# The output stage of a decoder step: injections computed ahead of the tile loop, half of the routed rows paired on GpSimd, a ring of hidden tiles

## The reference, cut to what matters

```python
idx = top_k(...)                                  # 8 of 64 experts for each row
h = h + routed(rmsnorm(h, g_ffn)) + shared        # routed: weighted sum of 8 expert rows
h = h + (p @ w_ple_proj) * sigmoid(rmsnorm(h, g_ple) @ w_ple_gate)
y = rmsnorm(h, g_final)
```

## Time and profile before

| | us |
|---|---|
| median of 3 runs (1900.89 to 1901.89) | 1901.25 |
| profiled execution, its own time | 1903.72 |
| span of the profiled execution, first to last instruction | 1901.9 |
| PE busy, whole span | 1716.1 (90%) |
| DVE busy, whole span | 968.8 (51%) |
| ACT busy, whole span | 779.8 (41%) |
| POOL busy, whole span | 513.7 (27%) |
| mean granted clock of TensorE, of 1 | 0.962 |

### The profile page before, as it was taken

One profiled execution on the slowest core, in us unless ns is written; L12 is line 12 of the kernel. 1 busy time (PEld: TensorE's weight loads), 2 busy tenths in 40 slices (PEclk: granted clock), 3 DMA queues, 4 the chain that ended last, 5 costly groups with the idle time before them and its releaser, 6 DMA issues. The chain is left out here.

```text
span 1901.9 us, 25091 instructions
## 1 busy us (share of the span) xinstructions
PE 1716.1 (90%) x7154; PEld 1075.3 (57%) x7155; DVE 968.8 (51%) x1639; ACT 779.8 (41%) x1453; POOL 513.7 (27%) x733
## 2 busy tenths in 40 slices
PE   6999999978985699999999998999999999937998
PEld 4666666545774456556656655656665565623443
DVE  3333333314996354555444545445555544637885
ACT  2222222212331355665555555545556554721221
POOL 0000110000665332333332334223333322411221
PEclk9999999987998799999999998999999999978999
DMA  9200000021111787888777768767787776958650
GB/s 360 100 0 0 0 0 0 15 96 47 67 67 62 255 294 257 274 286 292 255 243 248 257 232 299 246 228 271 260 280 274 260 253 222 337 219 331 270 166 28
DMA packets 124013, 363.70 MB, mean 191 GB/s; under 512 B 28966, under 2 KB 44262, under 8 KB 121389
## 3 DMA queue, kind: packets, MB, share of 16 engines
q1 hardware_dynamic: 87909, 290.85, 44.2%
q0 software_dynamic: 35760, 72.49, 10.7%
q10 hardware_dynamic: 320, 0.07, 0.0%
HBM read 334.52 MB, written 71.91 MB: 214 GB/s over the span
## 5 line engine op out<-in xcount | busy, mean ns | idle before, releaser
L1409 PE MATMUL Y<-raw_d,hT 128*128 128x512 f32 (+1 forms) x768 | 352.1, 602 | 19.7 <-ACT hT L1469 19.7
L197 DVE TENSOR_TENSOR lo_gu<-raw_g,hi_gu 128x1024 fp32r<-128x1024 f32 x130 | 153.5, 1221 | 366.5 <-ACT hi_gu L190 321.3
L1367 PE MATMUL GU<-hi_gu,x_hi 128*128 128x512 f32 (+1 forms) x768 | 322.0, 419 | 5.7 <-issue 4.1
L1367 PE MATMUL GU<-hi_gu,x_lo 128*128 128x512 f32 (+1 forms) x768 | 304.6, 397 | 0.0
L1367 PE MATMUL GU<-lo_gu,x_hi 128*128 128x512 f32 (+1 forms) x768 | 304.3, 396 | 0.0
L1477 ACT ACTIVATE y<-Y,w_t 128x512 f32<-128x512 f32 (+1 forms) x256 | 168.3, 683 | 238.5 <-PE Y L1409 230.6
L1328 POOL DMA_INDIRECT y_dram<-y,to_row x128 | 131.3, 1026 | 472.0 <-ACT y L1477 354.0
L1409 PEld LDWEIGHTS Y<-raw_d,hT 128*128 128x128 f32 (+1 forms) x768 | 132.3, 179 | 178.7 <-issue 167.3
L1317 POOL DMA_INDIRECT rows<-rows_dram,from_row x131 | 159.0, 1214 | 109.1 <-POOL from_row L1315 76.8
L1367 PEld LDWEIGHTS GU<-hi_gu,x_hi 128*128 128x128 f32 (+1 forms) x768 | 136.8, 178 | 77.4 <-issue 39.6
L107 POOL TENSOR_SCALAR st<-st 128x1 f32<-128x1 f32 (+3 forms) x45 | 14.4, 321 | 582.5 <-ACT junk L585 201.0
(11 more groups left out here) (221 smaller groups left out, 2139.3 us busy)
## 6 DMA issues: line engine op xcount, KB each, us to landing
raw_g<-in_w_exp_gate SPq DMA_DIRECT2D x130, 512.0 KB, 5.9
raw_u<-in_w_exp_up SPq DMA_DIRECT2D x130, 512.0 KB, 6.2
raw_d<-in_w_exp_down SPq DMA_DIRECT2D x130, 512.0 KB, 4.9
yk<-y_dram SPq DMA_DIRECT2D x16, 2048.0 KB, 12.7
rows_dram<-row SPq DMA_DIRECT2D x9, 512.0 KB, 2.7
h_dram<-resid SPq DMA_DIRECT2D x9, 512.0 KB, 2.7
w_big<-in_w_in SPq DMA_DIRECT2D x2, 2048.0 KB, 12.8
w_out<-in_w_out SPq DMA_DIRECT2D x1, 4096.0 KB, 18.1
```

Of the source, the lines that this page charges most:

```text
L197: dve.tensor_tensor(part_of(keep, "lo", m, par, h), part_of(keep, "raw", m, par, h), part_of(keep, "hi", m, par, h).bitcast(F32), ALU.subt ...
L1367: ins = pe.matmul(out, lhs[x], rhs[w], start=first and i == 0, stop=last and i == 2)
L1409: ins = pe.matmul(Y[half][0:n, :], hT[b][:, f, :], raw_d[par][:, f, cols], start=f == 0, stop=f == FC - 1)
```

## The change

- The two norm weights `g_ple` and `g_fin` get buffers that live from the expert stage on, and SyncE loads them at its head, ahead of `ple`; it waits for them at that stage's end.
- Injections: ahead of the tile loop TensorE transposes the p rows of all nine tiles straight from `ple` (no copy on GpSimd) and multiplies them; ScalarE copies each half product from PSUM into `inject`, which holds all tiles in SBUF. VectorE's multiply and add are then one whole tile wide each.
- Routed rows: GpSimd adds row 5 to row 4 and row 7 to row 6 of a tile, in place in `yk`; VectorE adds rows 0 to 3 and the two pairs: six adds.
- Hidden tiles: a ring of four buffers `res` in place of `resid4`, loaded tile by tile. `out`, `colT` and `pT` get two buffers each, sums of squares and roots a column per tile.
- ScalarE copies both halves of the transposed row. TensorE puts the transposes of t+1 between the two halves of the gate product of t. All loops are written out.

The diff, cut to its core (declarations, and what only renames, left out):

```diff
@@ build @@
-            keep["ple"] = ctx.enter_context(nc.sbuf_tensor("ple", [P, TILES, PLE], F32, side="right"))
+            for name, shape in (("ple", [P, TILES, PLE]), ("g_ple", [P, D]), ("g_fin", [P, D])):
+                keep[name] = ctx.enter_context(nc.sbuf_tensor(name, shape, F32, side="right"))
@@ experts, SyncE @@
-            for dst, src in ((ple[:, 0:PROMPT_TILES, :], a["p_prompt"][0, 0].rearrange("(t p) d -> p t d", p=P)),
+            for dst, src in ((keep["g_ple"][:], a["g_ple"][0:1, :].broadcast_to([P, D])),
+                             (keep["g_fin"][:], a["g_final"].rearrange("(a d) -> a d", a=1).broadcast_to([P, D])),
+                             (ple[:, 0:PROMPT_TILES, :], a["p_prompt"][0, 0].rearrange("(t p) d -> p t d", p=P)),
...
+            sp.wait_ge(keep["output_ld"], 16 * 4)
@@ output, SyncE @@
+            def hidden(t):
+                sp.dma_start(res[t % RING][:], tiles[t]).then_inc(h_ld[t % RING], 16)
...
+            hidden(0)
+            routed(0)
+            hidden(1)
+            routed(1)
+            hidden(2)
+            hidden(3)
+            for t in range(TILES):
+                if t + 2 < TILES:
+                    sp.wait_ge(summed, t + 1)
+                    routed(t + 2)
+                if t >= 2:
+                    store(t - 2)
+                    if t + 2 < TILES:
+                        hidden(t + 2)
@@ output, GpSimd @@
+            def pair_up(t):
+                pool_after(pool, keep["passed"], y_ld[t % 2][1], 16 * (t // 2 + 1))
+                for k in (TOP // 2, TOP // 2 + 2):
+                    pool.tensor_tensor(yk[t % 2][:, k, :], yk[t % 2][:, k, :], yk[t % 2][:, k + 1, :], ALU.add).then_inc(
+                        paired, 1)
...
+            pair_up(0)
+            norm_in(0)
+            pair_up(1)
+            norm_in(1)
+            for t in range(TILES):
+                if t + 2 < TILES:
+                    pair_up(t + 2)
+                if t:
+                    norm_out(t - 1)
+                if t + 2 < TILES:
+                    norm_in(t + 2)
@@ output, TensorE @@
+            ple_transposes(0)
+            for t in range(TILES):
+                if t + 1 < TILES:
+                    ple_transposes(t + 1)
+                project(t)
+            transposes(0)
+            for t in range(TILES):
+                gates(t, 0)
+                if t + 1 < TILES:
+                    transposes(t + 1)
+                gates(t, 1)
@@ output, ScalarE @@
+            p_copy(0)
+            for t in range(TILES):
+                if t + 1 < TILES:
+                    p_copy(t + 1)
+                j_copy(t)
+                if t == 4:
+                    square_sum(0)
+            col_copy(0)
+            square_sum(1)
+            for t in range(TILES):
+                if t:
+                    final_sum(t - 1)
+                if t + 1 < TILES:
+                    col_copy(t + 1)
+                sigmoid(t, 0)
+                if t + 2 < TILES:
+                    square_sum(t + 2)
+                sigmoid(t, 1)
@@ output, VectorE @@
+            def total(t):
...
+                for k in range(TOP // 2):
+                    own.did(dve.tensor_tensor(r[:], r[:], y[:, k, :], ALU.add))
+                    own.wait()
+                for i in range(2):
+                    dve.wait_ge(paired, 2 * t + i + 1)
+                    ins = dve.tensor_tensor(r[:], r[:], y[:, TOP // 2 + 2 * i, :], ALU.add)
...
+            total(0)
+            norm(0)
+            total(1)
             for t in range(TILES):
+                if t:
+                    add_injection(t - 1)
+                if t + 1 < TILES:
+                    norm(t + 1)
                 if t + 2 < TILES:
+                    total(t + 2)
+                if t:
+                    finish(t - 1)
```

More of the change, by code:

```diff
@@ L1602, in chosen_rows @@
                     sp.dma_start(yk[t % 2][0:n, k, :], chosen[t, 0:n, k, :]).then_inc(y_ld[t % 2][q], 16)
[L1604 to L1608, removed]
@@ L1674, in transposes, with gates @@
                     ins.then_inc(x_tr, 1)
[L1676 to L1684, removed]
-                    transposes(t + 1)
[L1686 to L1702, removed]
+            def gates(t, h):
+                after(pe, g_ready, 2 * t + h - 1)
+                for k in range(KC):
+                    if h == 0 and k % 4 == 0:
+                        pe.wait_ge(x_ev, 2 * t + k // 4 + 1)
+                    ins = pe.matmul(G[h][:], colT[t % 2][:, k, :], w_gate[:, k, h * 512:(h + 1) * 512],
+                                    start=(k == 0), stop=(k == KC - 1))
+                ins.then_inc(g_done, 1)
+            pe.wait_ge(zeroed, 2)
+            ple_transposes(0)
[7 more added lines that the diff above has]
+                if t + 1 < TILES:
+                    transposes(t + 1)
+                gates(t, 1)
         @block.scalar
@@ L1732, in _, with j_copy @@
[L1732 to L1738, removed]
+                after(act, j_done, 2 * t - 2)
+                act.activation(pT[t % 2][:].rearrange("p f q -> p (f q)"), XP[:, 0:PLE], ACT.Copy).then_inc(p_ev, 1)
+            def j_copy(t):
+                for h in range(2):
+                    act.wait_ge(j_done, 2 * t + h + 1)
+                    act.activation(inject[:, t, h * 512:(h + 1) * 512], J[h][:], ACT.Copy).then_inc(j_ev, 1)
@@ new lines, in col_copy, with sigmoid @@
+            def col_copy(t):
+                for b in range(2):
+                    act.wait_ge(x_tr, 2 * t + b + 1)
+                    if b == 0:
+                        after(act, g_done, 2 * t - 2)
+                    act.activation(colT[t % 2][:, 4 * b:4 * b + 4, :], X[b][:].rearrange("p (k q) -> p k q", k=4),
+                                   ACT.Copy).then_inc(x_ev, 1)
+            def sigmoid(t, h):
+                act.wait_ge(g_done, 2 * t + h + 1)
+                if h == 0:
+                    after(act, injected, t)
+                act.activation(gate[:, h * 512:(h + 1) * 512], G[h][:], ACT.Sigmoid).then_inc(g_ready, 1)
@@ L1767, in inject, with add_injection @@
[L1767 to L1776 removed]
+            def add_injection(t):
+                dve.wait_ge(g_ready, 2 * t + 2)
+                dve.wait_ge(j_ev, 2 * t + 2)
+                own.did(dve.tensor_tensor(inj[:], gate[:], inject[:, t, :], ALU.mult))
+                own.wait()
+                dve.tensor_tensor(res[t % RING][:], res[t % RING][:], inj[:], ALU.add).then_inc(injected, 1)
@@ L1778, in finish @@
             def finish(t):
                 dve.wait_ge(fin_ready, t + 1)
-                dve.wait_ge(out_st, 16 * t + 16)
-                dve.scalar_tensor_tensor(out=out[:], in0=resid[:, t, :], scalar=st[:, 5:6], in1=g_fin[:],
+                after(dve, out_st[t % 2], 16 * (t // 2))
+                dve.scalar_tensor_tensor(out=out[t % 2][:], in0=res[t % RING][:], scalar=rs[:, 1, t:t + 1], in1=g_fin[:],
                                          op0=ALU.mult, op1=ALU.mult).then_inc(out_ready, 1)
-            def following(t, first, between):
-                gather_sum(t, range(first, TOP), t % 2)
-                between()
-                norm(t)
-                col_copy(t)
```

165 lines of the change are left out of this document (61 added, 104 removed).

## The result

The changed kernel takes 1890.3 us (median of 11 runs, 1887.8 to 1897.2) against 1900.9 (median of 11, 1898.6 to 1903.9): a ratio of 0.995, 95% interval 0.994 to 0.996. It is faster, by 10.6 us; 1892.5 was forecast, within 1876 to 1906.

The account below looks back on a forecast made before the run. VectorE and GpSimd as a pair were to bound the changed tile loop: first gate product 1728.8, tiles through 1881.5, tail to 1891.6, clock 1.5, span 1893.1; plus 1.8 less 2.5 gave 1892.5 us, range 1876 to 1906.

Parts of the forecast that it names:

- The opening: Ahead of the tile loop: injection products made in idle time, first gate product at 1728.8, 6 us later, at full clock.
- The price of GpSimd's add: GpSimd's new two-input add of 128x1024 tiles in the output stage: 2.2 us taken, between 1.0 and 2.65.
- the sum: VectorE's steady tile, sum to sum: its operations, two stalls of 1.95 and 0.2 of small norms, 18.05 us.
- The path to SBUF: Output stage: one engine holds SBUF's path a whole instruction; each GpSimd add stalls VectorE 1.95 us, at injection add and row.
- The period: Steady output tiles: 18.05 us from sum to sum, 0.9 less than now, bound by VectorE and GpSimd as a pair.
- The clock: TensorE's clock may fall in its 3.3 us gaps, costing 2.7 us in a gate product; 1.5 us added in all.
- The tail: Behind the last gate product: sigmoid, multiply and add, square sum, norm, output and store, 10.1 us.
- Rival 1: Tile loop: GpSimd runs beside VectorE without stalls, TensorE's 14.7 us is the period; 1869.6 us, chance 0.13.
- rival 2: Tile loop: GpSimd's add costs more than its three streams; at 3.5 us an add, 1912 us; chance 0.14.
- rival 3: Tile loop: transfers bind, below 290 GB/s; 1896 us at 300 GB/s, about 1916 at 250; chance 0.05.
- rival 4: Opening: injections ahead don't hide, copies and transposes leave 1 us gaps per tile; 9 us later, 1901 us; chance 0.06.

Follow-up runs that it names:

- e3: Changed kernel with the norm weights g_ple and g_fin loaded late again, behind tile 0's routed rows; 1889.1 us, ratio 0.994 to the kernel before.
- e2: As e1, VectorE adding all eight rows, but GpSimd still makes two adds per tile into a spare tile nothing reads; 1907.6 us, ratio 1.004.
- e10: As e2, but GpSimd copies one routed row to the spare tile twice per tile instead of adding; 1886.9 us, ratio 0.993.
- e6: As e2, but GpSimd only sets the spare tile to zero twice per tile instead of adding; 1880.5 us, ratio 0.989.
- e1: Changed kernel with GpSimd's pair adds removed, VectorE adding all eight routed rows; 1880.1 us, ratio 0.988 to the kernel before.
- e7: Changed kernel with GpSimd adding none and rows 5 and 7 left out, so VectorE makes six adds; 1867.4 us, ratio 0.982.
- e4: Changed kernel with only tile 0's injection product made ahead, the others made in the tile loop; 1897.6 us, ratio 0.998.
- e9: e1 with small waits taken away, plus the row moved to ScalarE and g_ple multiplied into the gate weights once; 1872.8 us, ratio 0.985.

## Why the prediction was right

Point by point:

- *The opening.* First gate product 38.6 us into the stage forecast, 37.7 measured; that the early norm weights gain nothing, e3 shows.
- *The price of GpSimd's add.* 2.2 us taken between 1.0 and 2.65; 2.34 measured when VectorE rests. But the start-up taken off it, 0.25, is 0.3, and the sum uses only the difference: a stall of 1.95 forecast, 2.0 measured. That half of the price's error cancels is luck.
- *The path to SBUF.* That VectorE is shut out for a whole GpSimd instruction was inferred from small operations that waited themselves and one add that lost 0.07 us; e2 and e10 show it with its size. The Trainium skill's rule (SBUF — State Buffer, "SBUF: two separate sides"), which names a GpSimd operation that reads SBUF, is what e6 and e10 measured. The estimate of 2.25 us for the add, from the Trainium skill's GPSIMD Engine Reference, "Performance versus the Vector engine", was a little nearer to 2.34 than my 2.2.
- *The period.* 18.05 from sum to sum forecast. TensorE's transposes in the trace are 19.67, 18.16, 17.54, 18.13, 17.54, 18.13 and 14.67 apart, together 123.8 for the forecast's 19.1 + 90.5 + 14.7 = 124.3. That these agree is in part luck. With both stalls and no lateness of TensorE VectorE needs 17.54, half a microsecond less than the sum: no small norm of GpSimd stands in the way there (0.2 in the sum), and the output leaves 0.15 less between sum and multiply. e2, with two adds more, takes 17.54 + 2 x 1.26 = 20.06; 20.05 is measured. e1's period, too, was half a microsecond under its sum.
- *The clock.* The other three of these five tiles, at 18.13 and 18.16, are those in which TensorE was late. Behind a gap of 4.84 us it made the transposes in 1.97 and the product in 16.05 us (1752.81 above); behind one of 2.70 the next slow product takes 15.60 for 13.90, at a granted clock of 0.79 (mean of 1789 to 1797 us), and VectorE, which else waits 0.50 us for the sigmoid, waits 1.84:

```profile
1788.51 1.09 PE L1694 MATMUL OX<-ident,row 128*128 128x128 f32 x8 [2.70 <-DVE row L1801]
1789.43 15.60 PE L1703 MATMUL OG<-w_big,colT 128*128 128x512 f32 x32
```

```profile
1798.83 2.56 DVE L1809 TENSOR_TENSOR inj<-gate,inject 128x1024 f32<-128x1024 f32 x1 [1.84 <-ACT gate L1756]
1801.43 3.25 DVE L1811 TENSOR_TENSOR res<-res,inj 128x1024 f32<-128x1024 f32 x1
1804.60 1.98 DVE L1801 SCALAR_TENSOR_TENSOR row<-res,rs,g_ple 128x1024 f32<-128x1024 f32 x1
```

  Without the 1.70 us that the product lost, the wait would have been the usual 0.50, by an estimate from these rows. GpSimd's first add runs in that wait, so that the row is not stalled (1.98 here, 2.01 in the tile where VectorE waited 3.13), and the tile costs 0.6 more than 17.54 where TensorE's lateness is 1.1 to 2.6. Three such tiles are 1.8 us; the 1.5 added for the clock was about right, and so was its reason, that a late TensorE gives part of the stall back. The alternation itself the prediction saw only roughly.
- *The tail.* 10.1 forecast; from the last product's end at 1878.6 to 1888.6, 10.0.

Together: a stage of 202.9 forecast, 200.3 measured. The opening is 0.9 less, and the five tiles with the clock's term took 89.5 for 90.5 + 1.5; the first tile's 0.6 more goes the other way. That the median came out 2.2 us under 1892.5 is no finer than the scatter ahead of the stage.

Rival 1 fell to e2, rival 2 to the add's 2.34 us, rival 3 to e7 (14.61 a tile with the same transfers), rival 4 to the opening. What the prediction did not say, though its own numbers did: 1.26 us spared for 1.95 stalled is a loss, so this part of the change made the kernel slower by 13.5 us of stage (e1), and the rest of it faster by 24.9. Of that rest only the products ahead (e4) and the early norm weights (e3) were undone by themselves; what the ring, the second buffers, ScalarE's copies and the order on TensorE are worth each is open.

## What to carry to other kernels

Before giving VectorE's work to GpSimd, compare what it spares with what it stalls: while a GpSimd instruction read SBUF here, a VectorE instruction with two SBUF inputs waited for its end (2.0 us behind an add, 0.7 behind a copy). What cost nothing in these runs was GpSimd's work that fell into VectorE's own waits, and settings, which only write (e6). And when a change has several parts, price each by itself against the engine that is the bound after the others: here the gain of one hid the loss of another.

## What the runs showed of the hardware

- GpSimd's add of two 128x1024 float32 tiles takes 2.34 us (shortest in the changed kernel), a copy of one 1.03 (shortest in e10); two copies or two adds side by side with VectorE stall one VectorE operation each, by 0.7 and 2.0 us (e10, e2); two settings of the same tile (1.96 us for both) stall none and aren't stalled (e6).
- ScalarE's strided, scaled copy of 1024 columns takes 2.06 to 2.13 us (e9), twice its 1.06 for a square sum with the tile read in order; VectorE's strided row takes 2.0 where an operation in order takes 1.23 to 1.28.
- A VectorE multiply of 1024 float32 columns by one value per partition takes 0.70 us (eight in 5.60, e9), where one with two tiles as inputs takes 1.23.
